# Second output projection and last down projection by tokens, with row-sum norms turned back by TensorE

## What is computed

```python
h = rmsnorm(x, norm_mix_pre);  proj = h @ w_in          # 1024 -> 3080
...                                                     # differential attention, mLSTM
mixed = concat([o_diff, o_mlstm]) @ w_out               # 1024 -> 1024
x = x + rmsnorm(mixed, norm_mix_post)
h = rmsnorm(x, norm_mlp_pre)
u = square(relu(h @ w_up))                              # 1024 -> 4096
x = x + rmsnorm(u @ w_down, norm_mlp_post)              # 4096 -> 1024
```

## Time and profile before

| | |
|---|---|
| median of 3 runs | 1658.03 us (1657.59 to 1670.1) |
| profiled execution, its own time | 1658.36 us |
| span of its instructions | 1656.2 us |
| TensorE busy in the span | 1585.3 us (96%) |
| VectorE busy | 799.4 us (48%) |
| ScalarE busy | 575.5 us (35%) |
| GpSimd busy | 137.1 us (8%) |
| mean granted TensorE clock | 0.979 of full speed |

### The profile page before, as it was taken

How to read it: one execution, slowest core, us unless ns; L and a number is a source line. 1 busy time by engine, 2 the same in 40 slices (tenths; PEclk the granted TensorE clock), 3 DMA queues, 4 the chain that set the end, 5 groups by cost and what they waited for, 6 DMA issues and landing times.

```text
span 1656.2 us, 19483 instructions
## 1 busy us (share of the span) xinstructions
PE 1585.3 (96%) x7158; PEld 1279.5 (77%) x7158; DVE 799.4 (48%) x1128; ACT 575.5 (35%) x919; POOL 137.1 (8%) x106
## 2 busy tenths in 40 slices
PE   7999999999999999999999989899987899999997
PEld 5888888878767788888888767667776688888885
DVE  6444422455365564444224466597656543244333
ACT  5222221334255442323122352346533432234321
POOL 2000000011022110000000132000035000000010
PEclk9999999999999999999999999999998999999997
DMA  5333343333111133333333342211131233333331
GB/s 159 101 98 92 102 92 100 101 102 108 65 51 39 52 108 96 101 89 101 98 93 101 92 137 77 64 52 52 39 115 51 79 99 101 89 102 95 96 102 51
DMA packets 281175, 146.57 MB, mean 88 GB/s; under 512 B 19472, under 2 KB 277152, under 8 KB 280864
## 3 DMA queue, kind: packets, MB, share of 16 engines
q1 hardware_dynamic: 266400, 140.53, 29.2%
q10 hardware_dynamic: 14720, 5.32, 1.4%
HBM read 141.62 MB, written 4.21 MB: 88 GB/s over the span
## 4 chain that ended last, share of the span: by engine, by line
PE 84%; DVE 10%; ACT 3%; issue 2%; DMA 1%; POOL 0%; POOLq 0%; ACTq 0%; DVEq 0%; SPq 0%
PE bank L311 27%; PE bank L315 26%; PE bank L314 26%; DVE w_low L963 3%; DVE region L974 1%; ACT w_high L544 1%; ACT region L549 1%; PE bank L1843 1%; PE bank L1619 1%; PE bank L1608 1%; DVE region_f L1512 0%; ACT sq L557 0%; PE bank L1750 0%; DVE x L1515 0%; DVE d_s L1300 0%
## 5 line engine op out<-in xcount | busy, mean ns | idle before, releaser
L311 PE MATMUL bank<-region,w_high 128*128 128x512 f32 x1932 | 767.0, 397 | 35.5 <-DVE w_low L963 21.0
L314 PE MATMUL bank<-region,w_high 128*128 128x512 f32 x1932 | 756.5, 392 | 0.0
L315 PE MATMUL bank<-region,w_low 128*128 128x512 f32 x1932 | 756.4, 392 | 0.0
L311 PEld LDWEIGHTS bank<-region,w_high 128*128 128x128 f32 x1932 | 364.7, 189 | 130.3 <-DVE w_low L963 22.4
L315 PEld LDWEIGHTS bank<-region,w_low 128*128 128x128 f32 x1932 | 364.5, 189 | 78.6
L314 PEld LDWEIGHTS bank<-region,w_high 128*128 128x128 f32 x1932 | 365.0, 189 | 73.6 <-issue 0.2
L963 DVE TENSOR_TENSOR w_low<-w_raw,w_high 128x1024 fp32r<-128x1024 f32 (+1 forms) x259 | 340.6, 1324 | 58.7 <-ACT w_high L544 54.8
L544 ACT CAST w_high<-w_raw 128x1024 fp32r<-128x1024 f32 (+1 forms) x259 | 265.5, 1027 | 224.0 <-DMA w_raw<-in_ffn_w_down 106.9
L593 ACT CAST region<-ff_t 128x512 f32 (+1 forms) x76 | 47.3, 622 | 207.2 <-DVE ff_t L1006 203.5
L1003 DVE TENSOR_TENSOR ff_u<-bank,rstd 128x512 f32<-128x512 f32 x44 | 30.4, 692 | 154.8 <-PE bank L315 154.8
L1547 POOL TENSOR_TENSOR sq_sum<-sq_sum,sq 128x512 f32<-128x512 f32 x56 | 78.6, 1404 | 159.6 <-ACT sq L557 159.1
(11 more groups left out here) (231 smaller groups left out, 1084.7 us busy)
## 6 DMA issues: line engine op xcount, KB each, us to landing
w_raw<-in_ffn_w_down SPq DMA_DIRECT2D x48, 512.0 KB, 3.7
w_raw<-in_ffn_w_gate SPq DMA_DIRECT2D x44, 512.0 KB, 3.7
w_raw<-in_ffn_w_up SPq DMA_DIRECT2D x44, 512.0 KB, 3.7
w_raw<-in_w_in SPq DMA_DIRECT2D x40, 512.0 KB, 3.9
w_raw<-in_w_up SPq DMA_DIRECT2D x32, 512.0 KB, 3.9
w_raw<-in_w_down SPq DMA_DIRECT2D x32, 512.0 KB, 3.9
w_raw<-in_w_out SPq DMA_DIRECT2D x16, 512.0 KB, 3.9
region_f<-in_x SPq DMA_DIRECT2D x4, 512.0 KB, 5.9
```

Source lines behind the costliest of these rows:

```text
L311: mm = pe.matmul(out, a_hi, b_hi, start=start, stop=False)
L314: pe.matmul(out, a_hi, b_lo, start=False, stop=False)
L315: return pe.matmul(out, a_lo, b_hi, start=False, stop=stop)
```

## The change

1. `out2`, `f3_dn0` and `f3_dn1` hold a piece of the activations still (128 features by 128 tokens) and move 512 weight columns past it, so that results lie as 128 tokens by 512 features. The number and shape of the matmuls (three per step, 512 columns) stay. Blocks of weights are 2 x 128 rows by 512 columns.
2. The squares for these norms are summed along a row by ACT itself (`accum_out`, L987, L1049); `norm_stat`, `norm_spread` and POOL's sums of `post1`, `f3` and `post2` go. The `f3` norm is not multiplied into h: relu squared lets its factor out, and it is brought in with the last norm (`pre_q`).
3. x is turned into tokens by features during `dqk` and `dv` by 32 transposes (`turn_x`, `x_copy`), scaled there by the first block's last norm, and put by in that form. `rstd_fin`, its spread and POOL's multiplication go.
4. Behind `out2`, for every 128 tokens, TensorE turns x + norm(mixed) back into features by tokens: eight plain fp32 matmuls of x by the identity, and eight of `mixed` by an identity scaled by the norm (`turn_mixed`, `mix_ident`). ACT and DVE make its high and low parts (`mix_hi`, `mix_lo`).
5. The closing turn goes: DVE writes the result as tokens by features, SP stores it in eight pieces.
6. SP loads two rows of gains, spread over the partitions: `post_row` behind the `mv` blocks, `out_row` behind the first four `out2` blocks.

```diff
@@ dqk and dv, TensorE and ScalarE
+            def turn_x(g):
+                t_, half = divmod(g, 2)
+                ...
+                if g >= 2:
+                    pe.wait_ge(x_kept, g - 1)
+                for j in range(4):
+                    mm = pe.transpose(bank[4 + half][:, j * P:(j + 1) * P], x[:, 4 * half + j, t_ * P:(t_ + 1) * P], CI(C_IDENT))
+                mm.then_inc(x_turned, 1)
             def after_dqk(i):
                 if i >= 3:
                     swap_halves(i - 3)
+                if i >= 2:
+                    turn_x(i - 2)
...
                 if j == 2:
                     pe.wait_ge(g_rows, 1)
-                    pe.wait_ge(rstd_ready, SPREAD["m2"] + 2)
+                    pe.wait_ge(x_kept, 2 * TT)
@@ ACT, out2
+            split_hi(BLK["out2"] + 1 + AHEAD)
+            for t_ in range(TT):
+                act.dma_start(x_rows[:, t_, :], x_spill[:, t_, :]).then_inc(x_returned[t_], 16)
+            def mix_square(c, t_):
+                act.wait_ge(acc_ready, RES["out2"] + TT * c + t_ + 1)
+                ...
+                act.activation(sq[:, t_ % 2, :], out2_bank(c, t_)[:], ACT.Square, scale=float(D) ** -0.5,
+                               accum_out=mix_ss[:, c, t_:t_ + 1]).then_inc(token_sq, 1)
...
+            for j in range(3):
+                split_hi(BLK["out2"] + 4 + j)
+            for t_ in range(TT):
+                mix_square(0, t_)
+            split_hi(BLK["out2"] + 7)
+            for t_ in range(2):
+                mix_square(1, t_)
+                mix_deviation(t_)
+            mix_hi(0)
+            split_hi(BLK["f3_up0"])
+            mix_hi(1)
+            for t_ in range(2, TT):
+                mix_square(1, t_)
+                mix_deviation(t_)
+                mix_hi(t_)
+            split_hi(BLK["f3_up0"] + 1)
@@ DVE, f3_up: the norm is no longer multiplied in
-                            dve.scalar_tensor_tensor(ff_z[:, j % 2, :], bank[r % BANKS][:], 0.0, rstd[:],
-                                                     ALU.max, ALU.mult).then_inc(acc_free, 1)
+                            dve.tensor_scalar(ff_z[:, j % 2, :], bank[r % BANKS][:], 0.0, None, ALU.max).then_inc(acc_free, 1)
@@ DVE, the end
+            for t_ in range(TT):
+                out_sum(1, t_)
+                out_gained(1, t_)
+                dve.wait_ge(token_std, TOKEN_STD["out"] + t_ + 1)
+                link(dve.reciprocal(out_r[:, t_:t_ + 1], out_std[:, t_:t_ + 1]))
+                dve.wait_ge(acc_free, RES["f3_dn1"] + TT + t_ + 1)
+                out_final(1, t_)
+                out_final(0, t_)
@@ TensorE
+            def turn_mixed(t_):
+                pe.wait_ge(x_returned[t_], 16)
+                ...
+                if t_ >= 2:
+                    pe.wait_ge(xt_lo, GEN["f3"] + DT * (t_ - 1))
+                where = lambda n: bank[2 * (1 + t_ % 2) + n // 4][:, n % 4 * P:(n % 4 + 1) * P]
+                for n in range(DT):
+                    pe.matmul(where(n), x_rows[:, t_, n * P:(n + 1) * P], CI(C_IDENT), start=n % 4 == 0, stop=False)
+                pe.wait_ge(p_ident, t_ + 1)
+                for n in range(DT):
+                    mm = pe.matmul(where(n), mixed[:, t_, n * P:(n + 1) * P], mix_ident[:, t_ % 2, :], start=False, stop=n % 4 == 3)
+                mm.then_inc(p_turned, 1)
...
+            for t_ in range(2, TT):
+                for k in range(2, DT):
+                    out2_step(1, t_, k, k == 2 if t_ == 2 else k in (4, 6))
+                    if t_ == 2 and k == 4:
+                        turn_mixed(0)
+                    if t_ == 3 and k == 2:
+                        turn_mixed(1)
+            turn_mixed(2)
+            turn_mixed(3)
```

More of the change, by code:

```diff
@@ L923, in _ @@
-            split_hi(BLK["f3_up0"] + 2)
-            head("post1")()
-            for n in range(DT):
-                act.wait_ge(x_new, DT + n + 1)
-                residual(SQ["f3"], n, 6, part[1])
-            split_hi(BLK["f3_up0"] + 3)
-            up("f3_up0", part[0], False, head("f3"))
-            down("f3_dn0", 2)
-            up("f3_up1", part[0], False)
-            def last(n):
-                act.wait_ge(acc_free, RES["f3_dn1"] + n + 1)
-                square(SQ["post2"] + n, f3_sum[:, n, :])
@@ new lines, in _, with out_square @@
+            up("f3_up0", part[0], False, lambda: None)
+            for c in range(2):
+                f3_splits("f3_dn0", c, x_square_at if c == 0 else None)
+            up("f3_up1", part[0], False)
+            def out_square(c, t_):
+                act.wait_ge(o_sum, TT * c + t_ + 1)
+                act.wait_ge(token_sq, TOKEN_SQ["out"] + max(TT * c + t_ - 1, 0))
+                act.activation(sq[:, t_ % 2, :], f3_half(t_, c), ACT.Square, scale=float(D) ** -0.5,
+                               accum_out=out_ss[:, c, t_:t_ + 1]).then_inc(token_sq, 1)
@@ L1518, in _ @@
[L1518 to L1528 removed]
+            split_lo(BLK["out2"] + 1 + AHEAD)
@@ new lines, in _ @@
+            for t_ in range(TT):
+                x_add(t_)
+            up("f3_up0", part[0], False, lambda: None)
+            for c in range(2):
+                f3_splits("f3_dn0", c)
+                for t_ in range(TT):
+                    acc = f3_acc("f3_dn0", c, t_)
+                    dve.tensor_copy(f3_half(t_, c), acc[:]).then_inc(acc_free, 1)
+            dve.wait_ge(token_sq, TOKEN_SQ["x"] + TT)
+            link(dve.tensor_scalar(pre_ss[:], pre_ss[:], EPS, None, ALU.add))
+            link(dve.reciprocal(pre_q[:, 0, :], pre_ss[:]))
@@ L1653, in turn @@
                     side = 0
[L1654 to L1655 removed]
+                    if it is None and gated:
+                        side = 1
                         for k in range(DT):
@@ L2091, in _ @@
                     m_turn(k - 2)
-                side_by_side("out2", 3, k, mix2, mix2_in)
-            columns("out2", 8, mix2, first=3)
-            norm_stat("post1")
-            norm_spread("post1")
-            src = lambda k: parts(1, k)
-            up("f3_up0", src, False, "f3", norm_steps("f3"))
-            down("f3_dn0", 2, 0, HID["f3_up0"], HALF)
-            up("f3_up1", src, False)
-            down("f3_dn1", 2, 0, HID["f3_up1"], HALF)
-            norm_stat("post2")
-            norm_spread("post2")
@@ L2113 @@
+            for t_ in range(TT):
+                for k in range(12 if t_ < 2 else 8, HALF):
+                    if t_ == 0 and k % 2 == 0:
+                        block_ready(pe, b + k // 2)
+                    token_step("f3_dn1", 1, t_, k, False)
 _INS = ["x", "ffn1_norm", "ffn1_w_gate", "ffn1_w_up", "ffn1_w_down", "mix_norm", "w_in", "q_norm", "k_norm", "rel_bias",
```

355 lines of the change are left out of this document (265 added, 90 removed).

## The result

The changed kernel takes 1633.63 us, the median of 4 runs (1632.73 to 1635.89), the kernel before 1658.35 in the runs beside it. The ratio is 0.985, with a 95% interval of 0.9831 to 0.987: 24.7 us shorter, where 22 were forecast. The profiled execution took 1633.56 us, its span 1631.8.

The account below looks back on a forecast made before the run. TensorE, busy 96% of the span, was taken as the bound, with 36.6 us lost among its products and 23.8 behind them. 1658.4 - 17.2 - 7.0 + 2.0 = 1636.2, so 1636 us; 8 in 10 range 1625 to 1650.

Parts of the forecast that it names:

- the end: Behind the last matmul: 6.6 us remain against 23.8, as other pieces are done under the last group's matmuls; 17.2 saved.
- first to last matmul: From out2's first matmul to the last: losses of 29.6 us after against 36.6 before, 7.0 saved.
- waits after: TensorE's waits in that stretch after the change: 1.3 + 1.4 + 0.6 + 0.5 + 3.9 + 1.0 = 8.7 us.
- turn_mixed: Behind out2: 64 plain fp32 matmuls at 0.205 us plus edges add 13.5 us on TensorE's path (12.8 to 27).
- low clock: Behind group 3's wait: half a turn and 5.2 us of products at half speed, 4.2 us lost (0 to 7).
- dqk and dv: Turning x there: six of eight groups hidden, two cost 0.9 + 0.4, ACT's eighth copy 0.7; 2.0 us lost.
- group 3: In turn_mixed: its square stands behind mix_hi(2), so TensorE waits 3.9 us between the turn's halves.
- block 8: In out2: its split stands behind ACT's four squares and DVE's multiplications; wait 0.6 us, to 4 if x's loads delay it.
- 1728 x 0.2266: From out2's first matmul to the last: 1728 matmuls at the undisturbed stretch's 0.2266 us each, 391.6 us without losses.
- rival 3: The 960 moved matmuls are slower by tokens, 42 ns each: +40, 1676 us; decisive from 23 ns on; chance 0.04.
- case 1: Clock stays up or the walk is too strict: 4.2 us of low clock and some 3 of waits go; 1629; chance 0.14.
- Cases 2, 3 and 4: 2: dear turn, +12 or +15, 1650, chance 0.12; 3: rival 3; 4: end queues one group more, 1640, within forecast's 0.68.

Follow-up runs that it names:

- after: The changed kernel itself, first measurement and trace, against the kernel before: median 1633.63 us, ratio 0.985.
- after_again: The changed kernel measured and traced once more, nothing edited: 1634.31 us, ratio 0.9842.
- groups_together: Changed kernel with the last quarter of f3_dn1 running all four token groups side by side to the end: 1640.31 us, ratio 0.9895.
- x_turn_twice: Changed kernel with turn_x issuing its four transposes twice in dqk and dv: that stretch took 73.5 us; no whole time given.
- before_without_turn_back: Kernel before, without TensorE's last 32 transposes and ScalarE's copies, result stored by features: 1658.97 us in one run.
- square3_first: Changed kernel with group 3's square and root ahead of mix_hi(2), and its mix_scale ahead of mix_lo(2): 1633.24 us, ratio 0.9824.
- x_half_twice: Changed kernel with turn_mixed adding x twice (32 more plain fp32 matmuls): out2's first matmul to f3_up0's took 73.1 us; no whole time given.
- return_late: Changed kernel with ScalarE issuing the four loads of x behind the split of out2's seventh block: 1639.44 us, ratio 0.9888.
- square3_return_last: Changed kernel with group 3's squares first and the four loads of x behind the split of out2's eighth block: 1632.2 us, ratio 0.9839.
- square3_and_late: Changed kernel with group 3's square first and the loads of x behind the split of out2's seventh block: 1635.84 us, ratio 0.9855.

## Why the prediction was right

It came out 2.4 us above the median. The end, its largest term, was right by its mechanism; the rest came near by terms that were off both ways, which is partly luck. By its own terms:

| term | forecast | measured |
|---|---|---|
| the end | 17.2 saved (15.5 to 18) | 17.4 |
| first to last matmul | 7.0 saved | 4.7; over the four traces with the changed kernel's passage (after, after_again, groups_together, x_turn_twice) 4.7, 8.9, 8.8, 6.0: mean 7.1 |
| of it: waits after | 8.7 | 7.9, and 6.7 in after_again |
| turn_mixed | 13.5 | 14.5 |
| low clock | 4.2 | 3.3 here; 0, 0 and 1.6 in the other three |
| rest | 1.4 | 4.4, of which 3.0 in f3_up0 and f3_up1 |
| dqk and dv | 2.0 lost (-1 to 4) | about 0.9 lost |

*The end* was right piece by piece, within about 0.1 us but for what follows the last scaling (2.4 us, 2.8 forecast); its bounds weren't needed. groups_together shows that the order in which the groups end is part of it (8.3 us), and before_without_turn_back that the turn back by itself was 2.0 of the 17.4.

*Waits.* The walk named the right ones: 1.3 forecast and 1.1 for the first head, 1.4 and 0.99 for block 4, 3.9 and 3.0 for group 3, 1.0 and 0.9 at `f3_up0`; group 2's 0.5 was 0. The cause of the largest is shown by square3_first: the place of group 3's square behind `mix_hi(2)`. For block 8 the forecast was 0.6 with 4 as the bound if the loads of x delay it; measured were 1.9 and 0.7. It was not its own load that was late but block 7's, behind whose split ScalarE's four squares and block 8's split stand. In the three traces in which block 7's load took 7.3 to 7.5 us (after, square3_first, x_turn_twice) the wait was 1.9 to 2.0, in the three in which it took 6.0 to 6.2 (after_again, groups_together, x_half_twice) 0.6 to 0.8. return_late and square3_return_last show that the loads of x are what delays a block; without them beside it block 7's took 3.4 to 3.6.

*turn_mixed.* The mechanism was right and the price 8% low: 0.205 each where 0.223 was measured. I had read it from eight records (four matmuls) ahead of one product, which start 0.81 us ahead of it.

The four to one of the Trainium skill (TensorE: Matmul & The Clock Gate, Terms), from which I had worked out 0.44 each, isn't borne out: 0.223 against 0.109 from start to start for a transpose in the same kernel is a factor of two.

*Low clock.* The step that failed in detail: "A wait of 3.2 was enough to bring the clock down in the earlier trace rows, so I expect it here". In none of the six traces that have the wait for mix_ident (3.0 us in five, 1.2 in x_half_twice) did a low stretch follow it. Behind waits for weights of 4.4 and 4.8 us (return_late, square3_and_late), and behind all three of before's (3.1 to 4.9 us) in each of its three traces, one did. The wait for mix_ident stands between turns, those others ahead of products; whether its place or its length spared it was not tested. Of the shorter waits, that for block 8 had a low stretch behind it in all three traces in which it was 1.9 to 2.0 us and in none of the six in which it was 0.6 to 0.8; that of 0.5 at `out2`'s first matmul in two of eleven. In the first trace the sum was nearly right because such stretches came elsewhere, at 1201.9 and 1239.3; that is luck, and in after_again there was none.

*Rate.* "1728 x 0.2266" assumed that nothing changes the steady rate. It holds for the two down projections by tokens (0.2267 over the 384 steps of each), which settles rival 3: nothing of the 23 ns that it needed. But in `f3_up0` and `f3_up1`, whose products keep their form, the step is 0.2311, 768 times 0.0044 or 3.4 us lost (3.0 in the first trace and in x_half_twice, where `f3_up0` ran at 0.2300); the change has put four of their eight row tiles into f_rest. Nothing in the prediction looked there.

*dqk and dv.* From norm_stat(m2) to the turn of the gate rows, three traces of before took 71.1 us on average and ten of the changed part 71.9. The price of 0.44 per group held, to the second product behind a group, but more of it was hidden than I thought: the wait for rope_y fell by 0.4 and those for w_low by 1.1, and the one for ACT's eighth copy was 0.3 and not 0.7. The 2.3 us that the profiled execution gained upstream are mostly not the change: before had nine matmuls at half the clock at 560 us, in code that both share, and after had not. Over ten traces the first matmul of `out2` stands at 1204.6 (median), over three of before at 1204.2.

Of the rivals, case 1 (1629) came halfway: after_again's trace has neither a low stretch between `out2`'s first matmul and the last nor 2 us of the forecast waits, and that run took 1633.15, since the turn cost 1.0 and the rate 3.4 us more than forecast. The shortest run of the changed kernel was 1631.68. Cases 2, 3 and 4 did not occur.

## To carry to other kernels

Count an end piece by piece behind the last matmul: what is done for each tile behind a norm over the whole row costs once per tile, and tokens by features let all but the last group's be done under products. The order on the engines beside TensorE decides what remains: one square ahead of a group of copies was worth 3 us, and a load that must go somewhere should stand behind the last transfer that is wanted soon, not merely later (0 to 1.2 us gained here, 4.4 us of waiting when it only moved on to the next block). Where the runs of one kernel differ by 3 to 12 us, read an edit from the stretch that it touches, in several traces, and keep the median for the sum.

## What was not expected of the hardware

The same matmul, 128x512 in fp32r, starts every 0.2267 us with all its rows in region and every 0.231 with half of them in f_rest, in `f3_up1` of all eleven traces, whatever the order.

Beside the four loads of x (512 KB each) a weight block's load takes 6.0 to 8.3 us, where it takes 3.4 to 3.6 without them, and only the one block is touched. Among traces of the changed kernel it was 7.5 in one and 6.1 in the next; what sets it is open.

Low stretches of TensorE's clock (starts 0.43 apart, granted clock 0.50 to 0.52) come partly at fixed places (at 17 us in every trace) and partly not: in the changed kernel at 1201.9 and 1239.3 us in one trace, and at neither in the next, which has one at 1045. Most cost 0.8 to 2.6 us, and the runs of one kernel spread by up to 12 us (square3_first).
